# A mixture-of-experts step: one load queued without its wait for the first gather, and four register loads moved into a matrix product

## The reference, cut to what matters

```python
def moe_tokens(h, p):                       # h (T, 1024)
    scores = jax.nn.sigmoid((h @ p['w_router']).astype(jnp.float32))
    ...                                     # 8 experts of 64 are chosen for each token
    hg = jnp.einsum('td,edf->tef', h, p['w1'])
    hu = jnp.einsum('td,edf->tef', h, p['w3'])
    act = jax.nn.silu(hg) * hu * gate[:, :, None].astype(h.dtype)
    routed = jnp.einsum('tef,efd->td', act, p['w2'])
    shared = (jax.nn.silu(h @ p['ws1']) * (h @ p['ws3'])) @ p['ws2']
    return routed + shared
```

## Time and profile before

| | |
|---|---|
| median of 3 runs | 1293.77 us (1292.7 to 1294.26) |
| the profiled execution: its time | 1293.47 us |
| its span, first to last instruction | 1291.7 us |
| PE busy | 1228.1 us, 95% of the span |
| DMA engines, mean rate over the span | 261 GB/s |
| chain of work that ended last | PE 82%, DMA 6%, issue 5% |

### The profile page before, as it was taken

One profiled execution on the slowest core, in us unless ns is written; L12 is line 12 of the kernel. 1 busy time (PEld: TensorE's weight loads), 2 busy tenths in 40 slices (PEclk: granted clock), 3 DMA queues, 4 the chain that ended last, 5 costly groups with the idle time before them and its releaser, 6 DMA issues.

```text
span 1291.7 us, 26209 instructions
## 1 busy us (share of the span) xinstructions
PE 1228.1 (95%) x9291; PEld 919.6 (71%) x9292; DVE 469.9 (36%) x843; ACT 344.0 (27%) x626; POOL 369.7 (29%) x374
## 2 busy tenths in 40 slices
PE   5699999999999999978898999999799999999997
PEld 4599999999999999967755555555455555565552
DVE  0566686658666538127711111011001100110114
ACT  4332322322332631325311121121112112121212
POOL 1144544445457244310411221122022112212210
PEclk9799999999999999989999999999899999999999
DMA  9954263443421133308699999999999999999883
GB/s 307 285 165 148 82 207 102 146 146 92 152 65 49 44 104 93 120 1 327 277 363 362 340 343 419 389 419 419 418 417 418 395 403 358 417 419 412 343 340 141
DMA packets 157769, 337.31 MB, mean 261 GB/s; under 512 B 12390, under 2 KB 96870, under 8 KB 141328
## 3 DMA queue, kind: packets, MB, share of 16 engines
q1 hardware_dynamic: 140048, 295.55, 61.1%
q0 software_dynamic: 14256, 34.10, 7.0%
q10 hardware_dynamic: 3424, 7.09, 1.7%
HBM read 322.21 MB, written 33.30 MB: 275 GB/s over the span
## 4 chain that ended last, share of the span: by engine, by line
PE 82%; DMA 6%; issue 5%; DVE 2%; ACT 2%; POOL 2%; SPq 1%; ACTq 0%; DVEq 0%; POOLq 0%
PE ps L1648 26%; PE ps L1660 13%; PE ps L1430 9%; PE ps L1431 9%; PE ps L1432 9%; PE ps L1641 4%; PE ps L1373 2%; DMA w<-in_w_dram 2%; DMA ring<-in_w_ada_dram 2%; DMA h_rows<-ring 1%; PE ps L1727 1%; PE ps L1443 1%; PE ps L1654 1%; PE ps L1385 1%; PE ps L1735 1%
## 5 line engine op out<-in xcount | busy, mean ns | idle before, releaser
L1648 PE MATMUL ps<-w,xe 128*64 (+1 forms) x3136 | 352.6, 383 | 17.0 <-DMA w<-in_w_dram 9.1
L1648 PEld LDWEIGHTS ps<-w,xe 128*64 128x64 f32 x3136 | 228.5, 138 | 153.6 <-issue 50.1
L505 POOL TENSOR_TENSOR wsplit<-ring,wsplit 128x1024 fp32r<-128x1024 f32 x80 | 192.2, 2403 | 304.8 <-ACT wsplit L695 304.8
L1430 PE MATMUL ps<-h_s_hi,wsplit 128*128 128x260 f32 x960 | 272.2, 283 | 0.0
L1432 PE MATMUL ps<-h_s_hi,wsplit 128*128 128x260 f32 x960 | 270.7, 282 | 0.0
L1431 PE MATMUL ps<-h_lo_m_hi,wsplit 128*128 128x260 f32 x832 | 234.8, 282 | 0.0
L1308 DVE TENSOR_TENSOR rs<-sg,ps 128x128 f32<-128x128 f32 x98 | 23.8, 284 | 486.4 <-PE ps L1648 486.4
L1430 PEld LDWEIGHTS ps<-h_s_hi,wsplit 128*128 128x128 f32 x960 | 180.6, 188 | 6.7 <-issue 6.7
L1432 PEld LDWEIGHTS ps<-h_s_hi,wsplit 128*128 128x128 f32 x960 | 180.8, 188 | 0.0
L1660 PE MATMUL ps<-w,eactT 128*64 (+1 forms) x784 | 179.0, 598 | 0.0
L695 ACT ACTIVATE wsplit<-ring 128x1024 fp32r<-128x1024 f32 x80 | 84.8, 1060 | 311.4 <-PE ps L1432 295.4
(11 more groups left out here) (310 smaller groups left out, 1374.9 us busy)
## 6 DMA issues: line engine op xcount, KB each, us to landing
w<-in_w_dram SPq DMA_DIRECT2D x192, 1024.0 KB, 17.5
ring<-in_w_in_dram SPq DMA_DIRECT2D x56, 512.0 KB, 3.8
ring<-in_w_ada_dram SPq DMA_DIRECT2D x12, 2048.0 KB, 9.7
act<-y_rows SPq DMA_DIRECT2D x4, 2048.0 KB, 10.9
ring<-y_rows SPq DMA_DIRECT2D x4, 2048.0 KB, 16.4
ring<-in_w_out_a_dram SPq DMA_DIRECT2D x8, 512.0 KB, 3.5
ring<-in_w_out_b_dram SPq DMA_DIRECT2D x8, 512.0 KB, 3.7
ring<-in_w_o_dram SPq DMA_DIRECT2D x8, 512.0 KB, 3.5
```

Of the source, the lines that this page charges most:

```text
L505: pool.tensor_tensor(wsplit[:, b, 1], raw[raw_slot], wsplit[:, b, 0], ALU.subtract).then_inc(S["w_lo"], 1)
L1430: mm(ps[:, bank + h, 0:HT], wsplit[:, b, 0, k, :], hi[:, k, p:q], start=(k == 0), stop=False)
L1648: ins = mm(ps[a * STRIP:(a + 1) * STRIP, bank, 0:FE], xe[:, k, a * STRIP:(a + 1) * STRIP], w[a][:, k, :], start=(k == 0), stop=(k == C - 1))
```

## The change

It does two things. SP no longer waits for `xg_in` before it queues the three transfers of expert 4; the wait for `idx_mm` ahead of it stays. And PE's four register loads stand between the matmuls of the last piece of the shared expert's product, `shared_up(1, 1, 1)`: before its second, fourth, sixth and eighth matmul, the first of them behind a wait for `table_dve`. The `reg_mov` of `at_step` stays where it was.

```diff
             sp.wait_ge(S["idx_mm"], 1)
-            sp.wait_ge(xg_in, 16)
             up_weights(4, 5)
             down_weights(4, 5)
...
-            def shared_up(f, m, h):
+            def shared_up(f, m, h, between=None):
...
                 for k in range(C):
+                    if between and k % 2:
+                        between(k // 2)
                     ins = mm(ps[:, 2 * m + h, 0:HT], w[:, k, :], hT[:, k, a:b], start=(k == 0), stop=(k == C - 1))
...
             pe.wait_ge(S["sh_ev"], 2)
+            at_step = pe.alloc_register("step_pe")
+            entries = table[:, :, :].rearrange("a n e -> a (n e)")
+            next_at = pe.alloc_register("next_at_pe")
+            next_steps = [pe.alloc_register(f"next_steps_pe{n}") for n in range(3)]
+
+            def first_entry(n):
+
+                if n == 0:
+                    pe.wait_ge(S["table_dve"], 1)
+                    pe.reg_load(next_at, first_at[0:1, 0:1])
+                else:
+                    pe.reg_load(next_steps[n - 1], steps_of[0:1, n - 1:n])
+
             shared_up(1, 1, 0)
-            shared_up(1, 1, 1)
+            shared_up(1, 1, 1, first_entry)
...
             pe.wait_ge(S["early_dve"], 2)
-            at_step = pe.alloc_register("step_pe")
             pe.reg_mov(at_step, 0)
-            entries = table[:, :, :].rearrange("a n e -> a (n e)")
-            next_at = pe.alloc_register("next_at_pe")
-            next_steps = [pe.alloc_register(f"next_steps_pe{n}") for n in range(3)]
-            pe.reg_load(next_at, first_at[0:1, 0:1])
-            for n in range(3):
-                pe.reg_load(next_steps[n], steps_of[0:1, n:n + 1])
```

## The result

The changed kernel takes 1297.35 us (median of 12 runs, 1295.72 to 1298.73), the kernel before in the same job 1294.01. The ratio of the two is 1.0023, with a 95% interval of 1.0015 to 1.0030; that is 3.0 us by the ratio and 3.3 by the medians. I had forecast +0.7 us and a range up to 1296.4; the time lies 0.95 us above it, and the loss is over four times as large as forecast.

A forecast was written before the change was run, and what follows sets the result against it. PE, busy for 95% of the span, was taken as the bound. Loads -1.7, wait for the gather +2.3 and restart +0.1 gave +0.7 us: 1293.8 becomes 1294.5 us, range 1291.9 to 1296.4.

The forecast's parts named there:

- The four loads: Register loads leave the issue ahead of the first pass: -1.7 us; in the shared product, a bubble of 0 to 0.3.
- PE waits for the gather: Before the transposes: gather beside expert 4's weights takes 8.3 us, not 4.6; PE waits, +2.3 us, +0.1 for restart.
- The clock's part is nil: First pass: PE runs out of instructions anyway, so low clock costs nothing extra if it ends before the sequencer resumes.
- an up product that doesn't stand for code: Sign that the forecast is wrong: the first pass's up product runs without a stand for instructions.
- My rival: First pass: low clock of 3.5 us falls after 650.9, last 39 matmuls pay up to 1.7 us; total +2.4, 10%.
- So those waits move rigidly with PE: The two late waits for weights, at 906.74 and 925.10, shift with PE and gain nothing from earlier weights.
- passes from 660 on all later by the same 0.7: Expected sign: every pass after the first is delayed equally, by 0.7 us.
- something larger: A fetch like that at the 692.9 branch becomes longer or shorter by 2 us; chance 4%.
- Expert 4's weights have no waiter: No pass waits for expert 4's weights, so queueing them earlier returns nothing.
- what I had at 8%: Whole kernel slower by 2.6 us: low clock falling later in the first pass, together with a slow gather; 8%.
- The gather hardly suffers: Rival at the first gather: it takes 4.6 to 7 us, result -1.4 to -0.6 us; chance 20%.
- The wait for code goes away: Rival at the first pass: code fetched earlier, pass takes 7.1 instead of 9.5 us; result -1.4, chance 6%.

The follow-up runs named there:

- the second profile: The changed kernel run once more, unaltered, against the kernel before: median 1298.18 us, ratio 1.0028.
- its first half: Kernel before with only SP's wait for the first gather removed, register loads left in front of the loop: 1297.85 us, ratio 1.0022; repeated, 1297.11 us, 1.0025.
- the two shifted kernels: Changed kernel plus 90 small matmuls before the loop, with SP's wait for the first gather restored (ratio 0.9966) or replaced by one for the second (1287.34 us, 0.9946).

## Why the prediction was wrong, point by point

**The four loads** (-1.7). Right: the issue shrank from 3.27 to 1.59 us, and their new place cost 0.14 us in one profile and nothing in the other, within the 0 to 0.3 forecast.

**PE waits for the gather** (+2.3, and 0.1 for the restart). The mechanism was right and the term 0.8 us too small. The gather took 8.77 us, not 8.3. The transposes began at 11.31 against 8.37 (642.96 - 631.65, 640.32 - 631.95), +2.94, and took 1.15 us instead of 0.90, since PE came to them from a wait: +3.2 in all where I had +2.4. The first pass began 1.5 us later and not 0.7. That lies at my upper bound for the sum (+1.4), and would not have left the range.

**"The clock's part is nil".** This step failed, and with it the forecast. I let the low clock keep its length, 3.5 us, and set as a condition that it ends before the sequencer resumes. It did not: the clock fell where it fell before, but PE, now later, still stood, and the low clock lasted 6.8 us, from 645.3 to 652.1, past the sequencer's 651.3. In the first pass this made 0.37 us (0.7 in the second profile). My sign "an up product that doesn't stand for code" came true with it: PE did not run dry, and the gap near 650.9 is not there. My rival had the low clock come later and not longer, at up to 1.7 us and 10%.

**"So those waits move rigidly with PE", "passes from 660 on all later by the same 0.7".** The first is nearly right: the waits for weights shrank by 0.3 us each. But I carried it over to the fifth pass, whose standstill stands for code, and put its change at nothing. Its low clock doubled, 3.4 to 6.8 us, and its product took 1.10 us more (0.8 in the second profile), the largest part of what I missed. I had only "something larger", 4%, for this place, and there for a longer or shorter fetch.

The sum as it was: 1.5 + 0.4 + 1.1 = 3.0, and another 0.2 before the fifth pass that the later passes gave back. Of the 2.3 us beyond my 0.7, 0.8 are the gather and 1.5 the clock. The range had a slip as well: the 0.5 us for the scatter of medians would have put its upper end at 1296.2 + 0.5 = 1296.7, and I wrote 1296.4. The time lies above both.

**Expert 4's weights have no waiter.** Right: DMA stood idle at 652 to 655 instead of at 630 to 635.

**The rivals.** The outcome is closest to what I had at 8%, a low clock that costs more together with a gather over 8.5 us. "The gather hardly suffers" was wrong for 3 MB and would have been right for 1 MB. "The wait for code goes away" did not happen here; what shortens it is idle DMA or another place of the code.

What stays open: what sets the moment at which the clock falls. Given that moment, the profiles sort the 3.4 from the 6.8 us by whether PE had resumed. And the order of the effects in medians is known to some 0.1% only, so that the 1 us between the whole change and its first half is not resolved.

## What to carry to other kernels

A transfer that nobody waits for is not free to move forward: look at what else is in flight where it lands, and keep the backlog small enough to be through when the transfer on the path begins (here 1 MB was, 3 MB were not). A few us taken from a standstill are not yet won if the engine then stands for code, or if the clock's answer falls on other work; read the next two such places before you add up. And where loads have slack, later can be better than earlier: queueing the same weights 9 us later was worth 2 us with the loads as before and 5 us with the moved ones (ratios 0.9985, and 0.9966 against 1.0003). A good part of that is clock and not code: 8.81 us became 7.13 at the fifth pass in both, and why the clock stayed full there is not known.

## What the runs showed of the hardware

- Inside the first pass PE's sequencer stood for code 4.0 to 4.8 us while the DMA engines were full of weights, and 1.8 to 2.0 us while they were idle; at the branch ahead of it in the two shifted kernels it was 3.54 and 1.26 us. The Trainium skill (Runtime: NRT & Kernel Launch, "Instruction fetch mechanics") says that a taken branch breaks the sequential prefetch, and the stands here are all at or shortly after a branch past an expert without passes.
- 180 instructions more ahead of the loop moved these stands: one of 4 us moved to the branch before it, one of 5 us vanished, and the kernel became 4 us faster with 2.8 us more work.
- Standstills of 3.4 to 4.0 us before the same pass were followed by low clock of no length, 3.4 us, or 6.8 us: 7.13, 8.81 and 9.6 to 9.9 us for the same 64 matmuls. It was 6.8 us where the clock fell while PE still stood, and 3.4 us where PE's product had begun.
- The indirect gather of 0.5 MB took 4.6 us alone or with 1 MB just ahead, 7.0 with 2 MB, 8.5 to 8.8 with 3 MB.
